# Linear attention's row sums and one value copy moved in VectorE's order, with the prologue of transposed pieces two tiles ahead

## What is computed

```python
def adaln(c, w_ada, b_ada):
    m = jnp.einsum('bd,de->be', jax.nn.silu(c), w_ada) + b_ada
    return jnp.split(m, 6, axis=-1)
...
sh1, sc1, gt1, sh2, sc2, gt2 = adaln(cs[grp], w_ada[i], b_ada[i])
h = modulate(rms_norm(x, norm_mix[i]), sh1, sc1)     # h * (1 + scale) + shift
...
proj = jnp.einsum('btd,de->bte', h, w_in)            # gla_mixer
q, k, v, r, a_low = jnp.split(proj, [nq, 2 * nq, 2 * nq + nv, 2 * nq + 2 * nv], axis=-1)
logit = jnp.einsum('btr,re->bte', a_low, w_alpha) + b_alpha
g = jax.nn.log_sigmoid(logit.astype(jnp.float32)) / GLA_TAU
```

## Time and profile before

| | |
|---|---|
| median of 3 runs | 1394.04 us (1393.62 to 1394.4) |
| the profiled execution | 1394.21 us, its span 1392.3 us |
| PE busy | 1367.9 us, 98% |
| DVE busy | 948.0 us, 68% |
| ACT busy | 656.0 us, 47% |

### The profile page before, as it was taken

How to read it: one execution, slowest core, us unless ns; L and a number is a source line. 1 busy time by engine, 2 the same in 40 slices (tenths; PEclk the granted TensorE clock), 3 DMA queues, 4 the chain that set the end, 5 groups by cost and what they waited for, 6 DMA issues and landing times.

```text
span 1392.3 us, 26066 instructions
## 1 busy us (share of the span) xinstructions
PE 1367.9 (98%) x10754; PEld 1301.4 (93%) x10754; DVE 948.0 (68%) x1591; ACT 656.0 (47%) x1462; POOL 89.2 (6%) x149
## 2 busy tenths in 40 slices
PE   9999999999999999999999999999899999999999
PEld 6889889999999999999888888889899999999999
DVE  5678677579889788778765646576798653554554
ACT  5543444466553353251565655653665542552430
POOL 0000000200000000000300000000200000000000
PEclk9999999999999999999999999999999999999999
DMA  9644542244435444534423323112343222223222
GB/s 378 239 153 162 178 152 84 98 153 153 151 132 186 167 145 147 179 129 150 168 108 106 116 90 134 63 61 93 106 152 136 82 71 92 91 69 114 76 71 103
DMA packets 38013, 182.41 MB, mean 131 GB/s; under 512 B 4294, under 2 KB 6854, under 8 KB 26632
## 3 DMA queue, kind: packets, MB, share of 16 engines
q1 hardware_dynamic: 22984, 126.98, 26.0%
q0 software_dynamic: 14912, 53.78, 11.2%
HBM read 172.82 MB, written 7.91 MB: 130 GB/s over the span
## 4 chain that ended last, share of the span: by engine, by line
PE 89%; DVE 5%; ACT 3%; issue 2%; DMA 1%; POOL 0%; SPq 0%; DVEq 0%; POOLq 0%; ACTq 0%
PE ps L656 26%; PE ps L658 26%; PE ps L657 25%; PE ps L1054 2%; PE ps L1104 1%; DVE sq L1722 1%; DVE h_lo L1735 1%; PE ps L1013 1%; PE ps L1076 1%; ACT w_hi L1162 1%; PE ps L694 1%; PE ps L746 1%; PE ps L894 0%; DVE xT L1811 0%; DMA xT<-in_xT 0%
## 5 line engine op out<-in xcount | busy, mean ns | idle before, releaser
L658 PE MATMUL ps<-h_hi,w_lo 128*128 128x272 f32 x2048 | 592.2, 289 | 0.0
L656 PE MATMUL ps<-h_hi,w_hi 128*128 128x272 f32 x1952 | 569.5, 292 | 5.7 <-ACT up L1442 1.7
L657 PE MATMUL ps<-h_lo,w_hi 128*128 128x272 f32 x1952 | 561.4, 288 | 0.0
L658 PEld LDWEIGHTS ps<-h_hi,w_lo 128*128 128x128 f32 x2048 | 384.9, 188 | 0.0
L656 PEld LDWEIGHTS ps<-h_hi,w_hi 128*128 128x128 f32 x1952 | 367.4, 188 | 14.8 <-issue 4.9
L657 PEld LDWEIGHTS ps<-h_lo,w_hi 128*128 128x128 f32 x1952 | 367.8, 188 | 1.1 <-issue 1.0
L1162 ACT CAST w_hi<-w_raw 128x2048 fp32r<-128x2048 f32 (+2 forms) x106 | 179.2, 1691 | 193.7 <-PE ps L658 169.2
L1650 DVE TENSOR_TENSOR w_lo<-w_raw,w_hi 128x2048 fp32r<-128x2048 f32 (+2 forms) x105 | 215.1, 2049 | 63.5 <-ACT w_hi L1162 63.0
L657 PE MATMUL ps<-act_lo,w_hi 128*128 128x272 f32 (+1 forms) x704 | 203.8, 290 | 0.0
L656 PE MATMUL ps<-act_hi,w_hi 128*128 128x272 f32 (+1 forms) x704 | 203.5, 289 | 0.0
L658 PE MATMUL ps<-act_hi,w_lo 128*128 128x272 f32 (+1 forms) x704 | 203.2, 289 | 0.0
(11 more groups left out here) (289 smaller groups left out, 1769.9 us busy)
## 6 DMA issues: line engine op xcount, KB each, us to landing
w_raw<-in_wst SPq DMA_DIRECT2D x72, 1024.0 KB, 4.9
a_raw<-in_ada_r POOLq DMA_DIRECT2D x56, 512.5 KB, 4.7
w_raw<-in_wst SPq DMA_DIRECT2D x28, 768.0 KB, 4.3
a_raw<-in_ada_g POOLq DMA_DIRECT2D x24, 512.0 KB, 3.6
a_pro<-in_ada_p SPq DMA_DIRECT2D x8, 1024.0 KB, 16.5
v_raw<-in_wst SPq DMA_DIRECT2D x8, 1024.0 KB, 9.1
w_raw<-in_wst SPq DMA_DIRECT2D x10, 512.0 KB, 4.5
xT<-in_xT SPq DMA_DIRECT2D x4, 544.0 KB, 5.2
```

The source lines that it names most:

```text
L656: mm(out, lhs_hi, rhs_hi, start=first, stop=False)
L657: mm(out, lhs_hi, rhs_lo, start=False, stop=False)
L658: return mm(out, lhs_lo, rhs_hi, start=False, stop=last)
```

## The change

The prologue's sum over the four partial sums leaves PE: `ada_sel` becomes two plain transposes (128 columns each), and a DVE reduction (`tensor_reduce`) to `ada_sum` goes ahead of the bias. `ada_sel` of piece k+2 now stands at the end of tile k, where that of piece k+1 stood early in tile k. The high-by-low products leave `first_tile` as `low_products`: those of tile 0 stay in tile 0, those of tile 1 go to tile 2, and so on, one tile late; the last stand behind tile 7. DVE makes gain and scaled x of tile k+1 ahead of `h_lo` of tile k, and copies the first piece to SBUF in ACT's place. The first v unit goes to bank 6. In the heads two row sums of head 0 move from step 2 to step 1, the row sums of a step are spread over its units by a rounded-up quotient, and the first v unit of step 5 is copied out ahead of `decayed`.

```diff
-GLA_ROWS = [[0, 3, 3, 0, 0, 3, 3], [1, 3, 1, 2, 0, 3, 3], ...
+GLA_ROWS = [[0, 5, 1, 0, 0, 3, 3], [1, 3, 1, 2, 0, 3, 3], ...
@@ place_units
+        elif BL[n] == ("v", 0) and t == 0:
+            b = 6
@@ ada_sel (PE)
                 for t in range(2):
-                    ins = mm(ps[:, b, c + 2 * t:c + 2 * t + 2], a_part[:, i % 4, t * P:(t + 1) * P], sel[:, :], start=True, stop=True)
+                    ins = pe.transpose(ps[:, b, c + t * P:c + (t + 1) * P], a_part[:, i % 4, t * P:(t + 1) * P], ident)
@@ PE
+            def low_products(k):
+                pe.wait_ge(h_ok, k + 1)
+                for half in range(2):
+                    ins = mm(ps[0:2 * RANK, 4 + half, 0:HALF], aw_hl[:, k, :], h_lo[:, k, half * HALF:(half + 1) * HALF],
+                             start=False, stop=(k == KT - 1))
+                if k == KT - 1:
+                    ins.then_inc(alow_ok, 1)
+                for u in block_units(("qk", 0)):
+                    out, wh, wl, xh, xl = unit_terms(u, k)
+                    ins = mm(out, wh, xl, start=False, stop=(k == KT - 1))
+                    if k == KT - 1:
+                        ins.then_inc(unit_done, 1)
@@ first_tile (PE)
-                if turned is not None:
-                    ada_sel(turned)
                 if k == 0:
+                    ada_sel(1)
                     pe.wait_ge(aw_ok, 1)
...
-                if piece is not None:
-                    ada_mm(piece)
-                pe.wait_ge(h_ok, k + 1)
-                for u in us:
-                    out, wh, wl, xh, xl = unit_terms(u, k)
-                    ins = mm(out, wh, xl, start=False, stop=(k == KT - 1))
...
+                if k + 2 < NPRO:
+                    ada_mm(k + 2)
+                if k != 1:
+                    low_products(max(k - 1, 0))
+                if k + 2 < NPRO:
+                    ada_sel(k + 2)
...
             for k in range(KT):
-                first_tile(k, k + 1 if k + 1 < KT else None, k + 2 if k + 2 < KT else None)
+                first_tile(k)
+            low_products(KT - 1)
@@ ahead of the units of v of head 0 (PE)
+            pe.wait_ge(ada_ok, NPRO)
@@ ACT
-            part(0)
@@ ada_add (DVE)
-                TT(ada_pairs(ada)[:, :, i, :], ps[:, bank, c:c + 4].rearrange("p (t g) -> p t g", g=2), bias, ALU.add).then_inc(ada_ok, 1)
+                groups = ps[:, bank, c:c + 2 * P].rearrange("p (t j q) -> p t q j", t=2, j=4)[:, :, 0:2, :]
+                step.then(dve.tensor_reduce(ada_sum[:, i % 2, :, :], groups, AX_X, ALU.add))
+                TT(ada_pairs(ada)[:, :, i, :], ada_sum[:, i % 2, :, :], bias, ALU.add).then_inc(ada_ok, 1)
@@ prologue (DVE)
+            dve.wait_ge(ada_mm_ok, 1)
+            b_, c_ = product_at(0)
+            dve.tensor_copy(a_part[:, 0, :], ps[:, b_, c_]).then_inc(ada_part_ok, 1)
             gain_of(0)
...
-            for k in (1, 2, 3):
-                gain_of(k)
-                scaled(0, k, rms)
+            gain_of(1)
+            scaled(0, 1, rms)
+            for k in range(1, KT - 1):
+                gain_of(k + 1)
+                scaled(0, k + 1, rms)
++                if k == 3:
+                    dve.wait_ge(w_hi_ok, 1)
+                    TT(w_lo[:, 0, second_half], w_raw[:, 0, second_half], f32(w_hi[:, 0, second_half]), ALU.subtract).then_inc(w_lo_ok, 1)
                 modulated_lo(0, k)
@@ gla_slot (DVE)
-                def fill(step_):
+                def fill(step_, done=0):
                     rows = GLA_ROWS[h][step_]
-                    for _ in range(GLA_STEPS[h][step_]):
+                    n = GLA_STEPS[h][step_]
+                    for _ in range(n - done):
                         evacuate(next(todo), not (h == GH - 1 and step_ == 6))
-                        if rows:
+                        for _ in range(min(rows, -(-GLA_ROWS[h][step_] // n))):
                             ada_rows()
                             rows -= 1
...
+                early = min(GLA_STEPS[h][5], 1)
+                if early:
+                    evacuate(next(todo))
                 decayed(h + 1)
-                fill(5)
+                fill(5, early)
```

More of the change, by code:

```diff
@@ L70 @@
 _n = 0
-for _name, _k in [("ident", P), ("sel", 2), ("cmask", P), ("bones", P), ("selm", 2 * TS), ("fold", TS), ("smask", TS), ("isc0", 1), ("isc1", 1)]:
+for _name, _k in [("ident", P), ("cmask", P), ("bones", P), ("selm", 2 * TS), ("fold", TS), ("smask", TS), ("isc0", 1), ("isc1", 1)]:
     CST[_name] = (_n, _k)
@@ L398, in hybrid_stream_step @@
         vpart = lambda name: vec[:, VEC[name][0]:VEC[name][0] + VEC[name][1]]
-        ident, cmask, sel, bones, selm, fold, smask = (cpart(x) for x in ("ident", "cmask", "sel", "bones", "selm", "fold", "smask"))
+        ident, cmask, bones, selm, fold, smask = (cpart(x) for x in ("ident", "cmask", "bones", "selm", "fold", "smask"))
         c_vec = vpart("c").rearrange("p (k g) -> p k g", g=2)
@@ L795, in first_pair, with first_tile @@
                         units(us[6:8])
-            def first_tile(k, turned=None, piece=None):
+            def low_products(k):
[10 more added lines that the diff above has]
+                        ins.then_inc(unit_done, 1)
+            def first_tile(k):
                 us = block_units(("qk", 0))
-                cols = [slice(half * HALF, (half + 1) * HALF) for half in range(2)]
                 pe.wait_ge(h_hi_ok, k + 1)
@@ L810, in first_tile @@
                     mm(out, wh, xh, start=(k == 0), stop=False)
-                if turned is not None:
-                    ada_sel(turned)
                 if k == 0:
+                    ada_sel(1)
                     pe.wait_ge(aw_ok, 1)
                 for half in range(2):
-                    mm(ps[0:2 * RANK, 4 + half, 0:HALF], aw_hl[:, k, :], h_hi[:, k, cols[half]], start=(k == 0), stop=False)
+                    mm(ps[0:2 * RANK, 4 + half, 0:HALF], aw_hl[:, k, :], h_hi[:, k, half * HALF:(half + 1) * HALF], start=(k == 0), stop=False)
                 if k == 0:
@@ L823, in first_tile @@
                     mm(out, wl, xh, start=False, stop=False)
-                if piece is not None:
-                    ada_mm(piece)
-                pe.wait_ge(h_ok, k + 1)
-                for u in us:
-                    out, wh, wl, xh, xl = unit_terms(u, k)
-                    ins = mm(out, wh, xl, start=False, stop=(k == KT - 1))
-                    if k == KT - 1:
-                        ins.then_inc(unit_done, 1)
-                for half in range(2):
-                    ins = mm(ps[0:2 * RANK, 4 + half, 0:HALF], aw_hl[:, k, :], h_lo[:, k, cols[half]], start=False, stop=(k == KT - 1))
-                if k == KT - 1:
-                    ins.then_inc(alow_ok, 1)
-            pe.wait_ge(const_ok, 2)
+                if k + 2 < NPRO:
[4 more added lines that the diff above has]
+                    ada_sel(k + 2)
             pe.wait_ge(warm_ok, 4)
@@ L874, in keys_and_scores @@
                     pe.wait_ge(o_out, NR * h)
+                else:
+                    pe.wait_ge(*freed(v0[0]))
                 for r in range(NPR):
@@ L1854, in _ @@
             modulated_lo(0, 0)
[L1855 to L1869 removed]
+            gain_of(1)
[3 more added lines that the diff above has]
+                scaled(0, k + 1, rms)
+                if k == 3:
+                    dve.wait_ge(w_hi_ok, 1)
+                    TT(w_lo[:, 0, second_half], w_raw[:, 0, second_half], f32(w_hi[:, 0, second_half]), ALU.subtract).then_inc(w_lo_ok, 1)
+                modulated_lo(0, k)
             dve.wait_ge(next_hi_ok, 1)
             TT(w_lo[:, 1, first_half], w_raw[:, 1, first_half], f32(w_hi[:, 1, first_half]), ALU.subtract)
[L1872 removed]
+            modulated_lo(0, KT - 1)
             dve.wait_ge(w_hi_ok, 2)
@@ L2310, in _layout @@
     for q in range(2):
-        part("sel")[q::32, q] = 1.0
         part("bones")[q * HD:(q + 1) * HD, q * HD:(q + 1) * HD] = 1.0
```

15 lines of the change are left out of this document (2 added, 13 removed).

## The result

The changed kernel takes 1387.87 us (median of 5 runs, 1387.6 to 1388.13), the kernel before, run beside it, 1394.04 us. The ratio is 0.995, with a 95% interval of 0.9935 to 0.9965: 6.2 us faster, where 5.4 were forecast. The profiled execution took 1387.87 us as well.

A forecast was written before the change was run, and what follows sets the result against it. PE bounds the kernel, busy 1367.9 of 1392.3 us at full clock. Gains of 1.7 (prologue), 1.1 (head 0) and 2.6 us (heads 1 and 2) sum to 5.4, giving 1388.6 us, range 1387.4 to 1389.8.

The forecast's parts named there:

- everything behind head 2 is a chain through PE that moves as a whole: Behind head 2: time gained earlier is kept, since DVE's idle microseconds in each head let no debt carry; no loss counted.
- PE's own work in a tile is 3.55 - 0.12 = 3.43 us: Prologue tiles: PE's work per tile falls only by the turn's saving of 0.12 us, and PE stays the bound.
- The price of the turn: Prologue: two transposes cost PE 0.22 us instead of 0.34 for the `sel` matmuls, 0.84 us gained in seven tiles.
- The new waits: Ends of prologue tiles 0 and 1: PE waits 0.35 and 0.7 us, 1.05 lost together, bounds 0.5 and 1.8.
- The wait ahead of tile 7: Prologue: PE's wait of 0.86 us for ACT's `h_hi` shrinks to about 0.5, a gain of 0.36 us.
- the first turn: Prologue's first piece: idle DVE copies it instead of ACT, so the turn starts 0.25 us sooner.
- The first v unit: Prologue's end: with bank 6 free, PE's wait of 1.36 us for ACT goes; 0.1 us left over, gain 1.26.
- The loop's room: Prologue: the loop from turn through DVE and ACT to the next turn, 3.1 us, fits PE's 3.43 us tile by 0.3.
- (a): Rival: the reduction or DVE's wait on itself makes the loop exceed 3.43 us; prologue gives nothing, 1390.3 us; chance 0.16.
- A wait in the heads: PE's waits for DVE go, worth their idle time: head 0 gains 1.1 us, heads 1 and 2 1.3 each.
- (b): Rival, heads 1 and 2: the wait returns at the next copy, margin 0.4 us; if all returns, 1391.2 us; chance 0.09.
- (c): Rival, head 0: fifth row sum waits for its reloaded buffer (`a_raw`), deciding from 7.0 us landing; at 10 us, 1391.6; chance 0.05.

The follow-up runs named there:

- the two halves: `prologue_only`, the changed kernel with the heads as they were: 1392.25 us, ratio 0.9984; `heads_only`, the kernel before with the heads changed: 1389.14 us, ratio 0.9968.
- rows_only: The kernel before with head 0's row sums moved and the rounded-up spreading, without the copy ahead of `decayed`: 1392.6 us, ratio 0.9988.

## Why the prediction was right in its course, and which of its steps failed

The direction, the places and the order of the causes held: each forecast wait went or shrank where it was said to, no rival took over, and 1387.87 us lies in the range, nearer to its low end (worked out as the text says, from its own terms, the range is 1387.6 to 1389.9). Of the 5.4 us forecast, the ledger has 5.9 (2.19 + 1.39 + 3.15 - 0.80) and the medians 6.2; the difference between these two is within the spread of the runs. The terms it had gave 6.7, 1.3 more than it said, and a term that it put at nothing took 0.8 back. That the sum came so near is in part luck.

**The step that failed first: "everything behind head 2 is a chain through PE that moves as a whole".** It lost 0.80 us there, to the swapped banks. The prediction read the new bank as an edit of one unit and did not follow the counter behind it.

**The second: "PE's own work in a tile is 3.55 - 0.12 = 3.43 us".** It is 3.34. Four tiles, from the head of tile 2 to that of tile 6, took 14.25 us before (24.86 to 39.11) and 13.32 after (24.94 to 38.26): 0.93 us, where the term says 0.48. That is 0.45 of the 0.53 by which the prologue surpassed its forecast. The price of the turn was right: 0.22 us instead of 0.34 in the same view as the earlier trace rows. What was put at nothing, without a reason, is what the new order does to the neighbours: with the `aw` products ahead of the high-by-low ones the two cost 0.08 us less, and the first `aw` products cost 0.03 less. The other end of the bounds, a transpose at the price of `sel`, didn't come about: two cost 0.22 us in both places.

The Trainium skill (TensorE: Matmul & The Clock Gate, part 4), with about 275 ns for a transpose (of bf16; these are fp32), would have had the turns cost 0.55 us; they cost 0.22. As the length of one instruction its figure agrees with the trace of before, where each transpose of head 0 lasts 0.27 us; four of them together cost the chain 0.44, because they overlap.

**The new waits** in tiles 0 and 1 were put at 1.05 us together; PE's idle time there is 0.24 + 0.58 = 0.82, within the bounds of 0.5 to 1.8. The wait ahead of tile 7 shrank by 0.28 us instead of 0.36, and the first turn came 0.2 us sooner, for 0.25. The first v unit gave 1.33 by itself, for 1.26. These errors nearly cancel.

**The loop's room was put at 0.3 us and is about 0.05.** This didn't touch the sum, but it touched the chance of (a), which was closer to deciding than the prediction said. The loop before was measured from 25.52, which in the earlier trace rows is where the products ahead of the turn end. In PE's timeline of before the turn itself starts earlier:

```profile
25.36 0.50 PE L753 MATMUL ps<-cst,a_part 128*128 128x2 f32 x4
```

From there to the copy's end it is 3.07 us, not 2.91. DVE starts 0.42 us behind the turn's start instead of 0.54, 0.1 sooner as forecast, and the reduction adds 0.2: 3.16 us, which is what the changed kernel has (28.12 to 31.28). PE's tile is the 3.34 us above instead of 3.43, and the turn's weight load starts 0.12 us ahead of its matmuls, so 0.06 us are left. The reduction was right at 0.20. But the prediction was wrong to say that the trace has none: layer 1's softmax takes maxima with the same instruction. The groups of before, by shape (busy us, mean ns of one), have

```profile
L2103 DVE TENSOR_REDUCE nmx<-ps 128x1 f32<-128x32 f32 x4 | 0.7, 181 | 0.0
```

32 numbers per partition from PSUM in 0.18 us. With this row the upper bound of 0.42 us, which came from a copy, would have been needless. (What rival (a) takes from the Trainium skill, VectorE: DVE Perf Modes, stands there in "Rules for kernel authors"; here the reduction took 0.17 us, the addition of four numbers before 0.16.)

**A wait in the heads was put at its idle time and is worth 0.2 to 0.3 us more.** Heads 1 and 2 gave 1.58 and 1.57 us for 1.3 each, head 0 1.29 for 1.1. PE's timeline of before around one of these waits shows why:

```profile
132.88 0.28 PE L657 MATMUL ps<-w_lo,h_hi 128*128 128x256 f32 x1
133.00 0.28 PE L658 MATMUL ps<-w_hi,h_lo 128*128 128x256 f32 x1
134.59 0.38 PE L656 MATMUL ps<-w_hi,h_hi 128*128 128x256 f32 x1 [1.32 <-DVE v_r L1795]
134.82 0.28 PE L657 MATMUL ps<-w_lo,h_hi 128*128 128x256 f32 x1
```

Matmuls that follow one another start every 0.12 us and last 0.28. Without the wait the third row would start at 133.12: it is 1.47 us late, not 1.32. The matmul behind it starts 0.23 us later instead of 0.12, another 0.11. Together 1.58, what each head gave.

Rivals (b) and (c) kept their margins: 0.36 us from the end of the third copy to the start of the sample rows, for 0.4 forecast, and no wait for `a_raw`. That the heads' three edits stand apart from the prologue's is shown by the two halves, that the later heads' gain needs the copy by `rows_only`.

## What to carry to other kernels

Size a removed wait on PE from where the instruction would have started in the run of starts to where it did, not by the idle time shown. Take the prices of before and after from one view, and add up the whole tile, neighbours too, when the order changes. When a unit leaves a rotation of banks, keep the counter going or look up every place where the rotation meets a fixed bank. Where an experiment with one part of a change shows no gain, look for a new wait, in the weight loads too, before calling the part worthless: here the transposes in the old place had their whole gain taken by one.

## What the runs showed of the hardware

- Two transposes of 128 columns cost PE's chain 0.22 us among other matmuls at full clock, in either of two places, and four cost 0.44; one lasts 0.27 us. The two `sel` matmuls, which the traces show as four, cost 0.34.
- Behind the `sel` matmuls the four high-by-high products cost 0.60 us, behind transposes 0.51.
- A wait for an input can be hidden in PE's views and show at the weight load only: 0.18 us there was 0.15 us of the products' time in the chain.
- A reduction of 16 numbers per partition from PSUM takes DVE 0.17 us, as much as an addition of four; four in a row took 0.81 us.
- Two traces of the same program differ by about 0.5 us in where PE stands at a given instruction, so a ledger by marks tells steps of about 0.1 us only over short stretches.
